# Values of four heads in a block of their own in a gated recurrence layer

## The reference, cut to what matters

```python
zf_l, zb_l, i_l, q_l, g_l = jnp.split(h_lat @ w_in, idx, axis=-1)     # latent tokens
zf_c, zb_c, i_c = jnp.split(h_ctx @ w_in[:, :idx[2]], idx[:2], axis=-1)  # context: no q, no g
...
f = lb + (1.0 - lb) * jax.nn.sigmoid(zf)          # gates
k = (1.0 - lb) * jax.nn.sigmoid(-zf)
bc = jnp.cumsum(_chunks(logf), axis=2)            # logf = log(f)
k_dec = kc * jnp.exp(b_last[:, :, None] - bc)     # keys for the state
ds = jnp.einsum('bnchk,bnchv->bnhkv', k_dec, vc)  # state steps: keys (tokens) x values (tokens)
q_dec, k_inv = qc * jnp.exp(bc), kc * jnp.exp(-bc)
o = q_dec @ starts + where(mask, q_dec @ k_inv, 0) @ vc
y = (o_fwd + o_bwd) * rms * onorm_g * silu(g) @ w_out
```

## Time and profile before

| | |
|---|---|
| median of 3 runs | 2557.06 us (2555.89 to 2558.59) |
| the profiled execution | 2559.35 us, span of the core 2556.5 us |
| TensorE busy | 2509.0 us, 98% |
| VectorE busy | 1647.9 us, 64% |
| ScalarE busy | 1127.0 us, 44% |
| mean granted TensorE clock | 0.994 |
| the recurrence layer's projections | 815.3 to 1523.1 us of the span |

### The profile page before, as it was taken

The page is one execution under the profiler, slowest core; times in us unless marked ns, Lnnn a source line. Parts: engine busy times, 40 slices in busy tenths (PEclk is TensorE's granted clock), DMA queues, the critical chain, the costliest instruction groups (busy, mean ns, idle before and its releaser), DMA issues.

```text
span 2556.5 us, 34782 instructions
## 1 busy us (share of the span) xinstructions
PE 2509.0 (98%) x13215; PEld 2060.6 (81%) x13215; DVE 1647.9 (64%) x2404; ACT 1127.0 (44%) x1923; POOL 0.2 (0%) x4
## 2 busy tenths in 40 slices
PE   6999999999999999999999999999999999999998
PEld 2578888888887888888888887878888887987887
DVE  2368789788997545464645456657566757657674
ACT  3422122223225634353435346456455646555563
POOL 0000000000000000000000000000000000000000
PEclk8999999999999999999999999999999999999999
DMA  9975366656675523333332324666544465644453
GB/s 369 371 272 173 118 215 192 199 170 216 228 248 166 150 76 110 87 98 98 98 98 85 112 98 149 214 211 184 170 164 150 164 235 188 189 156 158 164 212 135
DMA packets 380893, 440.34 MB, mean 172 GB/s; under 512 B 23086, under 2 KB 254312, under 8 KB 378856
## 3 DMA queue, kind: packets, MB, share of 16 engines
q1 hardware_dynamic: 372544, 414.24, 50.1%
q10 hardware_dynamic: 8232, 24.52, 2.6%
HBM read 430.29 MB, written 8.41 MB: 172 GB/s over the span
## 4 chain that ended last, share of the span: by engine, by line
PE 94%; DVE 2%; ACT 2%; DMA 2%; issue 1%; ACTq 0%; DVEq 0%; SPq 0%
PE ps L1278 15%; PE ps L1279 15%; PE ps L1280 15%; PE ps L1281 13%; PE ps L1283 13%; PE ps L1282 13%; PE ps L1302 1%; DMA raw<-in_ada_w_dram 1%; PE ps L1955 1%; PE ps L1963 1%; DVE wl L2056 1%; PE ps L1658 1%; PE ps L1687 1%; PE ps L1650 1%; PE ps L1662 1%
## 5 line engine op out<-in xcount | busy, mean ns | idle before, releaser
L2056 DVE TENSOR_TENSOR wl<-raw,wh 128x1024 fp32r<-128x1024 f32 (+1 forms) x586 | 693.6, 1207 | 321.4 <-ACT wh L665 313.3
L665 ACT ACTIVATE wh<-raw 128x1024 fp32r<-128x1024 f32 (+1 forms) x586 | 597.5, 1045 | 617.5 <-PE ps L1280 232.4
L1278 PE MATMUL ps<-hTh,wh 128*128 128x512 f32 (+1 forms) x1820 | 681.4, 374 | 3.4 <-DVE wl L2056 1.9
L1279 PE MATMUL ps<-hTl,wh 128*128 128x512 f32 (+1 forms) x1820 | 673.9, 370 | 0.0
L1280 PE MATMUL ps<-hTh,wl 128*128 128x512 f32 (+1 forms) x1820 | 672.1, 369 | 0.0
L1281 PE MATMUL ps<-wh,hTh 128*128 128x512 f32 (+2 forms) x1568 | 615.9, 393 | 5.4 <-DVE wl L2056 3.1
L1283 PE MATMUL ps<-wh,hTl 128*128 128x512 f32 (+2 forms) x1568 | 605.4, 386 | 0.0
L1282 PE MATMUL ps<-wl,hTh 128*128 128x512 f32 (+2 forms) x1568 | 604.3, 385 | 0.0
L1278 PEld LDWEIGHTS ps<-hTh,wh 128*128 128x128 f32 x1820 | 342.8, 188 | 71.5 <-issue 7.5
L1280 PEld LDWEIGHTS ps<-hTh,wl 128*128 128x128 f32 x1820 | 342.1, 188 | 60.0
L1279 PEld LDWEIGHTS ps<-hTl,wh 128*128 128x128 f32 x1820 | 343.0, 188 | 58.9 <-issue 1.0
(11 more groups left out here) (310 smaller groups left out, 1883.3 us busy)
## 6 DMA issues: line engine op xcount, KB each, us to landing
raw<-in_ada_w_dram SPq DMA_DIRECT2D x96, 1024.0 KB, 5.8
raw<-in_w_in_dram SPq DMA_DIRECT2D x88, 1024.0 KB, 5.2
raw<-in_od_w_in_dram SPq DMA_DIRECT2D x256, 256.0 KB, 3.7
raw<-in_ev_w_in_dram SPq DMA_DIRECT2D x192, 256.0 KB, 4.2
raw<-in_w_out_dram SPq DMA_DIRECT2D x32, 1024.0 KB, 5.1
raw<-in_ev_w_out_dram SPq DMA_DIRECT2D x16, 1024.0 KB, 5.1
raw<-in_od_w_in_dram SPq DMA_DIRECT2D x16, 1024.0 KB, 5.1
raw<-in_od_w_out_dram SPq DMA_DIRECT2D x16, 1024.0 KB, 5.1
```

The source lines that it names most:

```text
L665: nc.scalar.activation(wh[:, ch.spl, part], raw[:, ch.raw, part], ACT.Copy).then_inc(s_hi, 1)
L1278: nc.tensor.matmul(out, w_h, x_h, start=first, stop=False, skip_group_check=True)
L1279: nc.tensor.matmul(out, w_h, x_l, start=False, stop=False, skip_group_check=True)
L2056: nc.vector.tensor_tensor(wl[:, ch.spl, part], raw[:, ch.raw, part], wh[:, ch.spl, part].bitcast(F32), ALU.subtract).then_inc(s_lo, 1)
```

## The change

The values of heads 4j+1 to 4j+4 get a block of their own (`v0` to `v3`), with the 128-token tiles stationary and 512 weight columns moving, ahead of the four head blocks, which now carry z, z and q alone (`LANES`: v0, h1, h2, h3, h4, v1, h5, ...). The values come out as tokens by features and are copied to `V4`; `v_turn`, `IT` and `V1` are gone. A head's split has 768 columns in a half chunk instead of 1024. As before, each block of TensorE projects one lane while the other engines process the lane before it; a values lane needs no processing but its four copies, which wait for `keep` of the head before. All blocks are written out instead of looped. A head's chunk is loaded with six DMAs instead of four, a values chunk with one. At the entry the units come in another order, and the first block is v0: half chunks 0 to 3 over the latent tokens, then over the context tokens, then both. In the gate stage the splits of chunks 8 and 9 stand ahead of the read-out's work.

```diff
+LANES = [x for j in range(4) for x in [("v", j)] + [("h", 4 * j + i + 1) for i in range(4)]]
...
-            ("hg", 16, [4] * 4),
+            *((f"{kind}{i}", 1, [1] * 4 if kind == "v" else [6] * 4) for kind, i in LANES),
...
-        UNITS = [(0, 0), (0, 1), (0, 2), (1, 0), (1, 1), (1, 2)] + [(v, i) for i in range(3, 8) for v in range(2)]
+        UNITS = [(v, i) for v in range(2) for i in range(4)] + [(v, i) for i in range(4, 8) for v in range(2)]
...
+            def load_values(j, c):
+                ch = st.chunk(f"v{j}", 0, c)
+                load(ch, [(slot4(ch), odw4[2, c][:, :, j * BLK:(j + 1) * BLK])])
             def load_head(h, c):
...
+                load(ch, [(slot3[:, t, :, f, :], odw4[a, c][:, 2 * t:2 * t + 2, (h - 1) * P:h * P]) for t in range(2) for f, a in enumerate((0, 1, 3))])
...
@@ ScalarE
...
+                kind, i = LANES[b]
+                hi(st.chunk(f"{kind}{i}", 0, p // 2), 4 * BLK if kind == "v" else 12 * P, halves=(p % 2,))
...
+            hi_lane(0, 1)
             unit(1)
             act.wait_ge(s_used, out0(15).piece(1))
             last_square(3, 4, SQ0, 0)
-            hi_head(0, 1)
             x_square(2)
+            unit(2)
+            hi_lane(0, 2)
             x_square(3)
+            unit(3)
+            hi_lane(0, 3)
+            for n in range(4, 8):
                 unit(n)
...
+            def move_values(j):
+                for t in range(4):
+                    nc.scalar.activation(V4[t], ps[:, t, :], ACT.Copy).then_inc(s_v, 1)
...
+                lane_done(b - 1)
+                if h:
+                    act.wait_ge(s_kdr, h * 2)
+                    for d in range(2):
+                        nc.scalar.activation(Z[:, d, :], ps[:, d, :], ACT.Exp, scale=-1.0).then_inc(s_hev, 1)
+                    nc.scalar.activation(Q, ps[:, 2, 0:SEQ], ACT.Copy).then_inc(s_hev, 1)
+                if past:
+                    keep(past)
+                if not h:
+                    if past:
+                        act.wait_ge(s_keep, past)
+                    move_values(LANES[b - 1][1])
                 split(1)
...
-            head(HEADS, gate_chunks)
-            gate_chunks(8)
+            block(len(LANES), gate_chunks)
+            hi(st.chunk("gate", 0, 8))
+            hi(st.chunk("gate", 0, 9))
             keep(HEADS)
             square_head(HEADS - 1)
             head_rms(HEADS - 1)
-            gate_chunks(9)
+            gate_sigmoid(1)
             gate_chunks(10)
+            gate_chunks(11)
             square_head(HEADS)
             head_rms(HEADS)
...
@@ TensorE
...
+            def values_project(j, p, tiles=range(4)):
+                ch = st.chunk(f"v{j}", 0, p // 2)
+                pe.wait_ge(s_lo, ch.half(p % 2))
+                for t in range(2):
+                    k = 2 * p + t
+                    w = slice((k % 4) * BLK, (k % 4 + 1) * BLK)
+                    for m in tiles:
...
+                        ins = three(ps[:, m, :], wh[:, ch.spl, w], wl[:, ch.spl, w], hTh[:, k, tok], hTl[:, k, tok], k == 0, k == KT - 1, False)
...
+            for p in range(4):
+                values_project(0, p, (0, 1))
+                if p == 0:
+                    unit_turn(3)
             unit_turn(4)
             unit_turn(5)
+            for p in range(4):
+                values_project(0, p, (2, 3))
+                unit_turn(6 + 2 * p)
+                unit_turn(7 + 2 * p)
+
+            def head_project(h, p):
...
+                    if k == 0 and h % 4 == 1:
+                        pe.wait_ge(s_v, h + f)
+                    elif k == 0:
+                        pe.wait_ge(s_hev, h * 3 - 5 + f)
...
-            def v_turn(h):
-                pe.wait_ge(s_hev, h * 4 - 1)
-                pe.wait_ge(s_sc, h * 2)
-                for t in range(4):
-                    ins = nc.tensor.transpose(pT[:, t * P:(t + 1) * P], IT[:, t * P:(t + 1) * P], ident)
-                ins.then_inc(s_vT, 1)
...
+            def block(b, chunk):
+                h = LANES[b - 1][1] if LANES[b - 1][0] == "h" else 0
                 for p in range(8):
                     chunk(p)
+                    if p == 6 and h:
                         k_turn(h)
+                if h:
+                    state_scores(h)
+                if h > 1:
                     head_sum(h - 1)
...
@@ VectorE
...
             dve.wait_ge(s_tile, 3)
             finish_tile(2, 4, X4, GB0, 13, late, XB0, 0)
-            lo_head(0, 0)
+            lo_lane(0, 0)
             low_unit(0)
+            lo_lane(0, 1)
             low_unit(1)
             dve.wait_ge(s_used, out0(15).piece(1))
             finish_tile(3, 4, X4, GB0, 13, late, XB0, 0)
-            lo_head(0, 1)
+            low_unit(2)
+            lo_lane(0, 2)
             x_root(2)
             x_scale(2, 0)
             x_scale(2, 1)
             x_root(3)
             x_scale(3, 0)
-            low_unit(2)
             x_scale(3, 1)
+            low_unit(3)
+            lo_lane(0, 3)
...
+                if past:
+                    states(past)
+                if not h:
+                    for p in range(1, 8):
+                        split(p)
                     return
                 denominators()
                 split(1)
```

More of the change, by code:

```diff
@@ L607, in _ @@
                     load_residual(u)
[L608 removed]
+            sp.wait_ge(s_plo, KT + 4)
             for c in range(2, 4):
[L610 to L611 removed]
+                load_values(0, c)
+            for kind, i in LANES[1:]:
                 for c in range(4):
[L613 removed]
+                    (load_values if kind == "v" else load_head)(i, c)
             w_gate = odw.rearrange("(c t p) n -> c p t n", t=4, p=P)
@@ L917, in keep @@
             def keep(h):
                 act.wait_ge(s_o, h * 2)
-                nc.scalar.activation(VP.rearrange("p (t v) -> p t v", t=2), V1[:, 0:2, :], ACT.Copy)
+                nc.scalar.activation(VP.rearrange("p (t v) -> p t v", t=2), VL[:, :, lane(h)], ACT.Copy)
                 nc.scalar.activation(QP.rearrange("p (d n) -> p d n", d=2), QD, ACT.Copy).then_inc(s_keep, 1)
-            def head(h, split, fin=True, moved=None, between=None):
-                split(0)
[L925 to L936, removed]
-                split(1)
[L939 to L945, removed]
@@ L1009, in _, with second @@
             act.wait_ge(s_plo, 2 * KT)
[L1010 to L1013, removed]
+            def second(p):
+                if p:
+                    hi_lane(1, p)
+                if p == 1:
+                    spread_gates(1)
+            block(1, second, sines)
+            for b in range(2, len(LANES)):
+                block(b, lambda p: hi_lane(b, p))
             x_rows = lambda t: x_save[t * P:(t + 1) * P, :]
@@ L1713, in _, with second @@
             nc.tensor.transpose(ps[:, 5, 0:2], posr, ident[0:2, 0:2]).then_inc(s_posT, 1)
-            def second_head(c):
-                head_proj(1, c)
-                if c == 1:
+            def second(p):
+                head_project(1, p)
+                if p == 1:
                     pe.wait_ge(s_gbe, 2)
-                if c == 3:
+                if p == 3:
                     pe.wait_ge(s_ang, 1)
-            head(1, second_head, fin=False)
-            with pe.Fori(2, HEADS) as h:
-                head(h, lambda c: head_proj(h, c))
+            block(1, second)
+            for b in range(2, len(LANES)):
+                kind, i = LANES[b]
+                block(b, (lambda p: values_project(i, p)) if kind == "v" else (lambda p: head_project(i, p)))
             def gate_turn(n):
@@ L1771, in out1_chunk @@
                         ins.then_inc(s_used, 1)
-            head(HEADS, gate_chunk)
+            block(len(LANES), gate_chunk)
             gate_chunk(8)
@@ L2617, in _, with block @@
             chunked = lambda x: x.rearrange("p (n c) -> p n c", c=CHUNK)
-            def head(h, split, comp=True, fin=True, between=None):
+            def block(h, past, split, between=None):
                 def bound(x, d):
@@ L2709, in head, with lane_block @@
                 k_move()
-            def head_chunks(h):
-                return lambda p: lo_head(h, p)
-            head(1, head_chunks(1), fin=False, between=angles)
-            with dve.Fori(2, HEADS) as h, step.loop(h, 2, HEADS - 2, 16):
-                head(h, head_chunks(h))
+            def lane_block(b, split, between=None):
+                h = LANES[b - 1][1] if LANES[b - 1][0] == "h" else 0
+                past = LANES[b - 2][1] if b > 1 and LANES[b - 2][0] == "h" else 0
+                block(h, past, split, between)
+            lane_block(1, lambda p: lo_lane(1, p), angles)
+            for b in range(2, len(LANES)):
+                lane_block(b, lambda p: lo_lane(b, p))
             def gate_product(n):
@@ L2742, in gate_chunks @@
                     gate_low(p // 4 - 1)
-            head(HEADS, gate_chunks)
-            head(HEADS + 1, lambda p: gate_chunks(8), comp=False)
```

(7 more changed lines are left out.)

200 lines of the change are left out of this document (92 added, 108 removed).

## The result

The changed kernel takes 2594.41 us (median of 4; 2591.82 to 2598.22), the kernel before 2557.82 beside it: ratio 1.0144 (95% interval 1.0132 to 1.0156), 36.6 us slower. The forecast was 2592 us (2574 to 2603). The profiled execution has a span of 2591.6 us, 35.1 more than before.

What follows compares the result with a forecast made beforehand. The prediction took TensorE, busy 98% of the span, as the bound. Its terms, +39.7 to the first gate matmul, -0.4 for the last value turn and -4.7 for the gate stage, add +34.6 to 2557.06: 2592 us, range 2574 to 2603.

Steps and rivals of the forecast that it cites:

- The step that carried it: Head blocks: VectorE's low splits of half chunks 1, 2, 5 end 4.9, 9.25, 21.0 us after the first projection matmul.
- The three stalls in such a block: TensorE waits 1.45, 0.85 and 1.35 us before half chunks 1, 2 and 5, in 8 head blocks.
- The sign that was named: In the trace after, TensorE's idle before projection matmuls grows from about 4 to about 45 to 50 us.
- The sum of the stalls: Head blocks, block starts and entry: stalls of 53.0 us against 4.1 before.
- The entry: First values block: waits of 2.3, 2.4 and 2.1 us, 6.8 against 3.3 of the same kind; its end at 872.5.
- Rival (c): Clock falls in new stalls, 1.6 us each, half of 12 blocks and twice at entry: +13, 2600 to 2605; chance 0.12.
- Second heads: Head 2 of each group, 4 blocks: 2.7 us of stall, 0.35 of it before half chunk 2; block 35.0 us.
- The gate stage: Splits 8 and 9 come first: 3.1 us of waits and 1.6 us of half clock go, -4.7 us.
- TensorE's own work: Recurrence layer: values projected in their own blocks, -2 us, and turns of values gone, -7 us: 9 us shorter without stalls.
- The margin of before: Kernel before: low split of half chunk 5 is ready 2.3 us before TensorE asks, with 0.95 us for the split.
- Nothing for written-out code, nothing for the DMAs: Written-out heads: 0, bounds 0 and 1.5 us gained; six smaller DMAs per chunk: 0, bounds 0 and +2 us.
- The sum: First gate matmul at 1562.8 instead of 1523.06, +39.7 us; with -0.4 and -4.7 in the gate stage, +34.6 in total.

Runs made afterwards that it cites:

- the three moves: Changed kernel with half chunk 5 split earlier (2579.26 us), half chunks 1 and 2 split earlier (2573.99 us), or both together (2561.99 us).
- e7_more_q: Changed kernel with queries projected for all 512 tokens instead of 256 in the head blocks, upper half unread: 2647.19 us.
- e6_gate_old: Changed kernel with the gate stage's order of the kernel before: 2598.20 us.
- e9_before_written_out: Kernel before with its three loops over heads written out, nothing else: 2557.14 us against 2557.49.
- e5_all: Changed kernel with splits 1, 2 and 5 earlier, head projections round four banks, context values copied before the readout's copies, and entry reordered: 2547.80 us.
- e3_both: Changed kernel with splits 1 and 2 right behind split 0 and split 5 behind split 4: 2561.99 us.
- e1_split5: Changed kernel with half chunk 5 split right behind half chunk 4, except in the gate stage's block: 2579.26 us.
- e10_before_gate: Kernel before with the new gate stage order alone: 2553.22 us against 2558.29.

## Why the prediction was right

**The mechanism.** The step that carried it, low(1), low(2) and low(5) ready at S+4.9, 9.25 and 21.0, came out at 4.86, 9.28 and 21.0. The three stalls in such a block, forecast 1.45, 0.85 and 1.35, are 1.46, 0.94 and 1.29 by the starts of the matmuls. The block of 36.2 is 36.24, the values block of 48.3 is 48.36, and a first and second head together, forecast 64.5, are 64.6 in two groups of three and 66.1 in the third, where the clock fell for some 3 us behind the 1.84 us wait for the values. The sign that was named, 45 to 50 us idle before projection matmuls, was missed: 41.4 are printed. The sum of the stalls, 53.0, counts them by the starts of the matmuls, where each is about 0.26 longer than printed. That they are late because of their place in the order, and not for any cost of the split itself, is shown by the three moves (-15, -20, -32), and that TensorE had time to spare there by the added queries.

**The entry.** Head 1 was to start at 873.4 us and starts at 872.67. In this execution the sum was right and its parts were not: the waits are 2.07, 0.65 and 2.16 (forecast 2.3, 2.4 and 2.1), and behind the first one the clock fell, so that half chunk 2 took longer and met split 3 nearly ready. In e7_more_q, whose entry is the same, the waits are 2.07, 2.23 and 2.15 as forecast, the clock falls one wait later, and head 1 starts at 873.84. Rival (c) had this mechanism; it came twice in the execution of the changed kernel, not in 8 places, and the entry took most of one back.

**Second heads.** I had 0.35 us before half chunk 2; there is none. Four times 0.35 is the only wait of the forecast that the trace doesn't have. The 35.0 for this block doesn't add up from its own terms either: 27.7 + 0.2 + 0.87 + 3.78 + 2.65 is 35.2.

**The gate stage.** Forecast -4.7; the spans of e6_gate_old and the changed kernel differ by 4.8, the medians by 3.8, and on the kernel before it is -5.1. The two waits in it are sure; the 1.6 us of half clock are luck in part. In the trace of e9_before_written_out the same wait, 1.95 us, was followed by a full clock (1.00 from 1581.0 to 1584.4).

**TensorE's own work.** The one term that was clearly off: -9 us in the layer, 2.25 a group. The groups without waits in e5_all show 1.4 a group, 5.5 in all. By the forecast's own terms a head block without stalls is 32.55 us; in e3_both it is 32.74. In the forecast of the whole this hardly shows, since it is added up from blocks.

**The margin of before.** The prediction puts it at 2.3 us, with 0.95 for the split. A split of 1024 columns takes 1.22, so low(5) ended at 1282.23 (1281.01 + 1.22), and TensorE took it up at 1284.39, 2.2 us later:

```profile
1284.39 0.40 PE L1278 MATMUL ps<-hTh,wh 128*128 128x512 f32 x1
```

The forecast of the block doesn't use this number.

**Nothing for written-out code, nothing for the DMAs.** The first is shown for the kernel before (0.9997). The second was not tried by itself. In e3_both no engine waits for a load of weights between 800 and 1640 us; the one wait for a DMA there is VectorE's for the positions, 1.4 us. That leaves little place for it.

**The sum.** Forecast +39.7 to the gate stage, measured 40.8. The entry and the first group came out 1.2 us short (the second values block starts at 1005.96, forecast 1007.2), the three groups behind them 2.3 long, 1.5 of it the half clock in one of them (66.1 against 64.6). From there to the end forecast -5.1, measured -5.7 by the spans. Total +34.6 forecast, +35.1 by span, +36.6 by median.

## What to carry to other kernels

An engine that is half busy can still set the pace: what counts is when each of its products is due, and that date moves when the consumer's block gets shorter. Before work is taken out of the bound engine's block, list for each product of the other engines its ready time and its due time in the new pitch; here the margin was 2.2 us and the block lost 11. The remedy was not less work but its place: splits moved into the time in which both engines waited for TensorE anyway gave back 32 of the 37 us, and a fourth bank in rotation with a split-up copy gave 10 more.

## What was not expected of the hardware

Single waits of about 2 us were followed by half the clock, but not each time. In the trace of the changed kernel a wait of 2.07 us (entry) and one of 1.84 us (for the values, at 1241.69) were followed by some 3.4 us at half clock, the 1.2 GHz level (0.58 and 0.57 granted over 4 us); behind the two other waits of 1.84 us and the one of 2.16 us it stayed full. Six of the kernels have the three waits of 1.84 us. The clock fell behind the middle one in four of them (the changed kernel, e1_split5, e6_gate_old, e7_more_q), and behind the first or the third in none. The entry of the kernel before, which has waits of 1.9 and 1.4 us, kept the full clock in its own trace and lost it in those of e9_before_written_out (0.57 from 819 to 823 us) and e10_before_gate (0.57 from 820 to 824), where the entry is the same code. Where nothing took it back a fall cost 1.5 us. Behind the waits for splits in the head blocks, at most 1.65 us long, it never fell in any of these traces. Why one wait is followed by a fall and another of the same length is not, these runs don't show.
